# The third expert's gate weights wait for the token rows of the second and third expert

## The reference

```python
def _hier_moe(u, p, l):
    g_logits = (u @ p['moe_w_group'][l] + p['moe_b_group'][l]).astype(f32)
    ...
    top_v, top_i = lax.top_k(e_in, TOP_K)          # 2 of the 4 experts of one of 4 groups
    ...
    hg = jnp.einsum('bld,edf->blef', u, p['moe_w_gate'][l])
    hu = jnp.einsum('bld,edf->blef', u, p['moe_w_up'][l])
    h = jax.nn.silu(hg) * hu * gates.astype(u.dtype)[..., None]
    return jnp.einsum('blef,efd->bld', h, p['moe_w_down'][l])
```

## Time and profile before

| what | value |
|---|---|
| median of 3 runs | 1241.03 us |
| lowest and highest run | 1240.05 and 1253.87 us |
| the profiled execution | 1254.41 us |
| its span, first to last instruction | 1252.6 us |
| PE busy | 1153.8 us (92%) |
| DVE, ACT, POOL busy | 375.7, 219.8, 141.3 us |
| moved by DMA | 340.96 MB, mean 272 GB/s |
| mean granted TensorE clock | 0.966 of full |

### The profile page before, as it was taken

One profiled execution on the slowest core, in us unless ns is written; L12 is line 12 of the kernel. 1 busy time (PEld: TensorE's weight loads), 2 busy tenths in 40 slices (PEclk: granted clock), 3 DMA queues, 4 the chain that ended last, 5 costly groups with the idle time before them and its releaser, 6 DMA issues.

```text
span 1252.6 us, 25009 instructions
## 1 busy us (share of the span) xinstructions
PE 1153.8 (92%) x10971; PEld 645.8 (52%) x10971; DVE 375.7 (30%) x962; ACT 219.8 (18%) x465; POOL 141.3 (11%) x163
## 2 busy tenths in 40 slices
PE   5999999899978999989999999999986999898997
PEld 2443445465654555545546665545664555454554
DVE  3202332573331111101156222587542121110114
ACT  2003211321311111111124111211031111111112
POOL 1143100112120000000010000132232000000001
PEclk9899999899988999989999999999998999899999
DMA  9988854369557999999957302001587799999984
GB/s 382 387 293 300 315 199 200 146 217 409 207 218 263 387 382 397 382 389 403 402 151 261 132 3 67 1 18 49 236 351 255 256 387 383 360 373 397 401 368 161
DMA packets 74716, 340.96 MB, mean 272 GB/s; under 512 B 6898, under 2 KB 17681, under 8 KB 59820
## 3 DMA queue, kind: packets, MB, share of 16 engines
q1 hardware_dynamic: 62872, 300.98, 62.8%
q0 software_dynamic: 11248, 37.99, 8.7%
q10 hardware_dynamic: 484, 0.35, 0.1%
HBM read 315.02 MB, written 24.27 MB: 271 GB/s over the span
## 4 chain that ended last, share of the span: by engine, by line
PE 68%; DMA 19%; DVE 7%; issue 2%; ACT 2%; POOL 1%; SPq 1%; POOLq 0%; DVEq 0%; ACTq 0%
PE ps L2269 18%; PE ps L1980 17%; DMA ring<-in_moe_w_up 12%; PE ps L1902 11%; PE ps L2293 7%; PE ps L2493 3%; DMA ring<-in_ada_w 3%; PE ps L1923 2%; DMA work<-x_rows 2%; PE ps L2202 2%; PE ps L2252 2%; PE ps L2463 1%; PE ps L2279 1%; PE ps L1895 1%; DMA x_rows<-work 1%
## 5 line engine op out<-in xcount | busy, mean ns | idle before, releaser
L2269 PE MATMUL ps<-ring,work 128*32 128x256 f32 x5248 | 329.2, 394 | 34.9 <-DMA ring<-in_moe_w_up 30.7
L2269 PEld LDWEIGHTS ps<-ring,work 128*32 128x32 f32 x5248 | 164.9, 113 | 144.9 <-issue 48.8
L1980 PE MATMUL ps<-uT,ring 128*128 128x384 f32 x640 | 216.9, 496 | 2.4 <-DVE uT L1330 1.3
L1980 PEld LDWEIGHTS ps<-uT,ring 128*128 128x128 f32 x640 | 121.7, 194 | 87.7 <-issue 10.4
L2293 PE MATMUL ps<-ring,work 128*32 128x256 f32 x1792 | 106.6, 379 | 0.8 <-DVE work L1748 0.8
L1748 DVE COPY work<-ps 128x128 f32<-128x128 f32 x82 | 23.9, 291 | 254.0 <-PE ps L2279 253.9
L1902 PE MATMUL ps<-ring,uT 128*128 128x512 f32 x192 | 84.1, 595 | 0.0
L1154 ACT ACTIVATE work<-ps 128x128 f32<-128x128 f32 x82 | 22.8, 277 | 348.7 <-PE ps L2269 348.7
L2293 PEld LDWEIGHTS ps<-ring,work 128*32 128x32 f32 x1792 | 57.5, 110 | 39.5 <-DVE work L1748 1.2
L1744 DVE TENSOR_TENSOR work<-ps,work 128x128 f32<-128x128 f32 x82 | 23.9, 292 | 170.6 <-ACT work L1154 170.6
L890 POOL DMA_DIRECT2D work<-x_rows x30 | 15.6, 520 | 435.9 <-PE ps L2252 425.0
(11 more groups left out here) (348 smaller groups left out, 1075.3 us busy)
## 6 DMA issues: line engine op xcount, KB each, us to landing
ring<-in_moe_w_gate SPq DMA_DIRECT2D x32, 2048.0 KB, 11.5
ring<-in_moe_w_up SPq DMA_DIRECT2D x32, 2048.0 KB, 18.0
ring<-in_ada_w SPq DMA_DIRECT2D x24, 2048.0 KB, 11.3
ring<-in_moe_w_down SPq DMA_DIRECT2D x22, 2048.0 KB, 19.7
uT<-in_moe_w_down SPq DMA_DIRECT2D x10, 1536.0 KB, 19.1
ring<-in_rec_w_in SPq DMA_DIRECT2D x6, 2048.0 KB, 24.0
ring<-in_hy_w_in SPq DMA_DIRECT2D x6, 2048.0 KB, 11.2
y_rows<-work SPq DMA_DIRECT2D x72, 96.0 KB, 11.0
```

What stands on the lines that cost most here:

```text
L1980: ins = pe.matmul(bank(key)[0:rows, 0:T], w(k), uT[:, k, :], start=(k == 0), stop=(k == DC - 1))
L2269: ins = pe.matmul(bank(key)[32 * q:32 * q + 32, 0:2 * P].rearrange("p (a n) -> p a n", a=2), xg[:, u, k, 32 * i:32 * i + 32], ring[:, 3 * ...
```

## The change

In `step(0)` of both layers SP waits, behind the wait for the first expert's last `gate_up`, for two more things ahead of issuing the third expert's gate weights: that the first row load of the layer on `rows1_loaded` has landed (the second expert's rows), and that on `rows0_loaded` (the third expert's). For layer 0 these counts are 16 and 16. For layer 1 they are 16 x 9 and 16 x 8, since a layer has eight loads on the first and seven on the second.

```diff
                     full(sp, (l, p, "GU", TILES[p] - 1))
+                    if p == 0:
+                        sp.wait_ge(S("rows1_loaded"), 16 * (l * (NE // 2) + 1))
+                        sp.wait_ge(S("rows0_loaded"), 16 * (l * (NE // 2 - 1) + 1))
                     load_part(0, e, u)
                     load_part(1, e, u)
                     if p != AHEAD:
```

## The result

The changed kernel has a median of 1235.34 us in 20 runs (1232.88 to 1240.0), the kernel before, in 20 runs beside it, 1244.07 us (1234.13 to 1253.87). The ratio is 0.9943, with a 95% interval of 0.9927 to 0.9958: about 7 us less by the ratio and 8.7 by the medians, where 12.4 were forecast. The second thing to see is the spread: 20 us before, 7 us after.

What follows compares the result with a forecast made beforehand. Each mixture was taken as bound by TensorE's chain, then the DMA engines; the smaller term, the stream's 6.2 us per layer, counted: 12.4 us off 1241.03 gives 1228.6 us. Likeliest case's range 1225 to 1235, overall 1223 to 1242.

Steps and rivals of the forecast that it cites:

- What bounds the kernel, and the wait: Each mixture: TensorE's chain first, then DMA; rows slowed beside third expert's weights leave TensorE idle 7.24 and 8.48 us.
- Part 1: Start of each mixture: second expert's rows alone land 4.7 us after issue, gate weights issued at 373.5 and 963.7.
- Part 2: TensorE's first transposes after the row wait: 8.6 us earlier in layer 0, 6.1 to 8.4 in layer 1, clock included.
- Part 3: DMA stream up to the fourth expert's gate weights: 7.34 MB at 377 GB/s, starting 6.2 us earlier in each layer.
- The rival that gave TensorE's chain the end: DMA has slack in later weight waits, so TensorE's whole 17.0 us comes through: 1224.0 us; chance 0.15.
- Part 4: Transfers SP holds behind the new wait: up weights, fourth expert's down weights, first expert's stores; costs nothing.
- The sum: Both layers: 6.2 + 6.2 = 12.4 us, taken from the median 1241.03 to give 1228.6 us, 1.0% less.
- The stream gives nothing: Rival: DMA queue worked off only 0.6 us earlier, TensorE waits longer at 466; 1 us gain, 1240; chance 0.17.
- slower: Rival: row loads slow by themselves, weights issued only when third expert's rows land; 6.4 us late per layer, 1253.9; chance 0.08.
- The wait is no wait: Rival: SP isn't held, or the rows gain nothing for another reason, without a loss: 1241 us; chance 0.05.
- the likeliest case: Both layers start the weight stream 6.2 us earlier: 1228.6 us, own range 1225 to 1235; chance 0.55.

Runs made afterwards that it cites:

- the forced kernels with the wait in one layer: Kernel before, POOL holding each layer's first row load until the first expert's last gate_up, SP's wait in one layer: layer 0 1246.67 us, layer 1 1247.33 us.
- the kernel with the order fixed: Kernel before, with SP waiting until POOL has issued both row loads, not for them to land: 1239.73 us, ratio 0.9950.
- the forced pair: Kernel before, POOL holding each layer's first row load until the first expert's last gate_up: 1255.04 us without SP's wait, 1237.08 us with it in both layers.

## Why the prediction was off

**What bounds the kernel, and the wait: right for the execution that was profiled.** The idle time, its cause and its place are as read. That execution lost the race in both layers; at 1254.41 us it was slower than each of the three runs known.

**Part 1, the landing: right, a little pessimistic.** 4.0 us in both layers, forecast 4.7; the gate weights 5.15 and 5.25 us after the row loads, forecast 6.0. The Trainium skill's fit (DMA: Bandwidth & Descriptors, "Anatomy of one DMA — SWDGE (gpsimd) path") gave 2.9 us as an estimate; the trace has 4.0 for the load, so the fit is too small here.

**Part 2, TensorE: right, 1 us too small in each layer.** The fourth expert's gate weights are asked for 9.5 and 9.4 us earlier, counted from the row loads; forecast 8.6 and 6.1 to 8.4. The clock stayed up in both layers of the changed kernel, over an idle time of 1.78 us too. That is not safe to count on: where SP waits for the second expert's rows alone, the clock fell in layer 0 behind an idle time of 0.90 us and the half tile took 3.47 us, and in the changed kernel itself it took 3.61 us behind one of 1.75 us (the third line of TensorE's timeline above). The length of the idle time alone did not decide it.

**Part 3, the stream of weights: the term that was mis-sized, in layer 1.** "6.2 us" for each layer. From the issue of its row loads to the six ScalarE instructions of L1142 ahead of the next mixture, layer 0 is 562.8 us with the collision (mean of five profiles, 561.8 to 563.6) and 556.4 with the wait (six, 554.2 to 558.8): 6.4. From the row loads to the end, layer 1 is 294.3 and 284.2 (five and six profiles): 10.1. So by the traces one layer came out as forecast and the other with TensorE's whole gain. (The medians of the forced kernels with the wait in one layer, 8.4 and 7.7 us, don't show this split; that stays open.) At the gate weights that SP issued at 1057.01 before and 1042.46 after, among the first late ones of layer 1, the gain had shrunk to 6.4 us, as the sum has it (the row loads themselves were 8.19 us earlier, which is taken off), and by 1094.99 against 1077.08 it was back at 9.7. Why it comes back is not settled. The rival that gave TensorE's chain the end, 17.0 us, was the right size for an execution with the collision in both layers, 18.0. I had read a DMA share of 1.0 as proof that nothing else can set the end.

**Part 4: right.** Nothing held back was missed.

**The sum: the step that failed.** "I take the difference as the same and set it against the median." The profile was one end of a spread, and a good part of the spread was the effect itself. With the collision in both layers the wait is worth 18.0 us. Where the rows lead by 4 us or more it is worth nothing (ratio 1.0011 on the chip with the pauses, for the wait on the second expert's rows). Where they lead by 0.4 to 1.3 us it is worth some 4 us: the execution that won the race took 1239.65 us and the kernel with the order fixed 1239.73, against 1234.48 and 1235.94 for the change beside them. On the chips without pauses the medians of the kernel before, 1244.1 to 1246.3, lie about half way between 1235 and 1255, and the change gains 7 to 11 us by the ratios: 0.9943, 0.9937, 0.9916 and 0.9918 in four comparisons. How many executions lose in both layers, in one, or in none was not counted; of the four profiled there three lost in both and one in none, and with the loss forced in one layer the kernel took 1247, which is near these medians. I had noted the 13.4 us between the profile and the median and passed over it as noise, while 14.7 us is what lies between two executions on one chip of which one lost the race in both layers and the other won it.

**The rivals.** "The stream gives nothing" and "slower" are excluded by the forced pair: 4.0 us of landing behind the wait, not 6.9, and no row load slow by itself. "The wait is no wait" had chance 0.05 and holds, in part of the executions. The time, 1235.3, lies within the wide range of 1223 to 1242 and just above the likeliest case's own 1225 to 1235, but for a reason that isn't in either.

## What to carry to other kernels

If single runs of a kernel differ by as much as a suspected wait, look at several profiles before subtracting that wait from the median: a wait may be the outcome of a race between two queues, and then a fix gains in the median only about its price times how often the race is lost. Where a small transfer that an engine waits for and a large one that nobody needs yet are issued within a microsecond on two queues, fix the order; waiting for the small one to land left the DMA engines half empty for some 5 us here, and cost nothing because they had a gap later. The order alone gave 6 of 10 us here; the wait for the one load that TensorE needs first was as good as waiting for both.

## What the runs showed of the hardware

A 384 KB row load took 3.7 to 4.8 us where the weights were issued 3.9 us or more behind it, and 10.6 to 11.8 us when 4.2 MB of weights were issued within 0.1 us of it or up to 1.8 us ahead of it. Between the two lies a steep edge: with the weights 0.04 us behind, it took 11.0 us; 0.42 us behind, 5.7; 0.53 behind, 4.6; 0.89 behind, 3.9. The second row load, issued half a microsecond after the first, still took 12.1 and 11.6 us in the cases of 0.42 and 0.53. The Trainium skill has the DMA engines alternate between queues packet by packet (DMA: Bandwidth & Descriptors, "Queues, rings and completion order"). That agrees with a load that is slowed and not held back altogether, but it doesn't say that half a microsecond of lead halves the time.

On one chip TensorE's matmuls of the first expert came in groups of five with pauses while the scatter ran, 10.8 us for 128 of them, in four profiles of four and in both layers; in the sixteen other profiles the same 128 matmuls took 7.11 us without a pause. Fourteen of these are of three other chips; for the first profile of either kernel the chip is not on record. The same four profiles are the ones with 6 us more at the end, while the experts' results are gathered. What holds the engines up there was not tried.
